# Routing of two expert layers: sums copied by columns ahead of the statistics, choice and counting by block, block 1's shift behind the placing

## What is computed

```
x = layer_norm(ALPHA * x + mixed @ w_o[layer], ln_mix_g[layer], ln_mix_b[layer])
# hier_moe(x):
probs_g = softmax(x @ w_group + b_group)              # 4 groups; the best one is taken
logits_e = (x @ w_router + b_router).reshape(T, 4, 4)
in_group = logits_e of the chosen group; softmax; top 2 of its 4 experts
gates = p_group * p_expert / (sum of the two), for 2 of the 16 experts
out = sum over experts of gate * (silu(x @ w_gate[e]) * (x @ w_up[e])) @ w_down[e]
x = layer_norm(ALPHA * x + out, ...)
```

## Time and profile before

| | us |
|---|---|
| median of 3 runs | 897.98 (897.81 to 900.09) |
| the profiled execution, its own time | 899.86 |
| its span, first to last instruction | 898.1 |
| PE busy | 879.3 |
| DVE busy | 494.2 |
| ACT busy | 406.5 |
| POOL busy | 32.3 |
| granted TensorE clock, mean | 1.000 |

### The profile page before, as it was taken

The page is one execution under the profiler, slowest core; times in us unless marked ns, Lnnn a source line. Parts: engine busy times, 40 slices in busy tenths (PEclk is TensorE's granted clock), DMA queues, the critical chain, the costliest instruction groups (busy, mean ns, idle before and its releaser), DMA issues.

```text
span 898.1 us, 13388 instructions
## 1 busy us (share of the span) xinstructions
PE 879.3 (98%) x5344; PEld 670.3 (75%) x5344; DVE 494.2 (55%) x740; ACT 406.5 (45%) x559; POOL 32.3 (4%) x73
## 2 busy tenths in 40 slices
PE   8999999999999999999999999999999999999998
PEld 7988998954543699878545445898878888888887
DVE  4798877611111775525211117656568777767566
ACT  4755655332221636653322216345646555565441
POOL 8000010000000000000000000000000000000010
PEclk9999999999999999999999999999999999999999
DMA  9924416969999494329599994654534555546611
GB/s 318 321 96 141 142 47 242 368 234 411 409 409 403 150 315 154 107 81 363 187 411 410 409 403 159 209 183 138 202 126 162 190 187 187 187 141 234 236 45 48
DMA packets 102829, 205.80 MB, mean 229 GB/s; under 512 B 6896, under 2 KB 57840, under 8 KB 102768
## 3 DMA queue, kind: packets, MB, share of 16 engines
q1 hardware_dynamic: 101184, 202.14, 62.7%
q10 hardware_dynamic: 1584, 2.81, 0.8%
HBM read 203.87 MB, written 1.05 MB: 228 GB/s over the span
## 4 chain that ended last, share of the span: by engine, by line
PE 85%; DVE 6%; ACT 3%; issue 2%; DMA 2%; SPq 1%; DVEq 0%
PE psum L723 82%; DVE w_lo L2233 2%; DMA raw<-in_a_w_in 1%; ACT w_hi L1702 1%; ACT arena L1702 1%; SPq L373 1%; DMA x_res<-in_x 1%; ACT x_slots L1702 0%; PE psum L1560 0%; PE psum L851 0%; PE psum L1247 0%; DVE xt L2254 0%; PE psum L967 0%; PE psum L1063 0%; PE psum L842 0%
## 5 line engine op out<-in xcount | busy, mean ns | idle before, releaser
L723 PE MATMUL psum<-xt,w_hi 128*128 128x256 f32 (+1 forms) x1056 | 256.2, 323 | 2.6 <-DVE w_lo L2233 1.3
L2233 DVE TENSOR_TENSOR w_lo<-raw,w_hi 128x2048 fp32r<-128x2048 f32 x88 | 200.6, 2288 | 45.9 <-ACT w_hi L1702 45.7
L723 PE MATMUL psum<-xt,w_lo 128*128 128x256 f32 x704 | 198.4, 282 | 0.0
L723 PEld LDWEIGHTS psum<-xt,w_hi 128*128 128x128 f32 x1056 | 177.3, 190 | 20.5 <-issue 1.8
L1702 ACT ACTIVATE w_hi<-raw 128x2048 fp32r<-128x2048 f32 (+1 forms) x90 | 169.8, 1892 | 36.8 <-PE psum L723 21.2
L723 PEld LDWEIGHTS psum<-xt,w_lo 128*128 128x128 f32 x704 | 134.0, 190 | 0.0
L723 PE MATMUL psum<-w_hi,xt 128*128 128x512 f32 (+1 forms) x336 | 103.8, 380 | 0.7 <-DVE w_lo L2233 0.4
L1702 ACT ACTIVATE arena<-psum 128x512 f32<-128x512 f32 (+2 forms) x74 | 43.2, 601 | 109.9 <-PE psum L723 81.6
L723 PE MATMUL psum<-hi_as_raw,x_slots 128*64 128x512 f32 x176 | 80.8, 596 | 0.0
L723 PE MATMUL psum<-lo_as_raw,x_slots 128*64 128x512 f32 x176 | 80.8, 596 | 0.0
L723 PEld LDWEIGHTS psum<-w_hi,xt 128*128 128x128 f32 x336 | 61.3, 189 | 12.6 <-issue 1.8
(11 more groups left out here) (279 smaller groups left out, 1260.4 us busy)
## 6 DMA issues: line engine op xcount, KB each, us to landing
hi_as_raw<-in_gate_up SPq DMA_DIRECT2D x44, 512.0 KB, 8.0
lo_as_raw<-in_gate_up SPq DMA_DIRECT2D x44, 512.0 KB, 9.6
raw<-in_ffn_w_up SPq DMA_DIRECT2D x44, 512.0 KB, 4.6
raw<-in_gate_up SPq DMA_DIRECT2D x40, 512.0 KB, 7.2
raw<-in_a_w_in SPq DMA_DIRECT2D x26, 512.0 KB, 7.0
raw<-in_w_down SPq DMA_DIRECT2D x24, 512.0 KB, 11.0
raw<-in_attn_w_in SPq DMA_DIRECT2D x24, 512.0 KB, 5.8
raw<-in_ffn_w_down SPq DMA_DIRECT2D x22, 512.0 KB, 4.2
```

What stands on the lines that cost most here:

```text
L723: return pe.matmul(o, l, r, start=start, stop=stop, skip_group_check=skip)
L2233: return dve.tensor_tensor(w_half(h, w_lo), w_half(h, raw), w_half(h, w_hi).bitcast(F32), ALU.subtract).then_inc(lo_split, 1)
```

## The change

Sums: ACT copies each half of a block as soon as PE has made it (`o_done` for block 0, `half_used` for each half of block 1), and DVE takes the statistics from the copy in SBUF. Scaling goes by halves. Choice: `choose(b)` runs for each block by itself. Counting: `count_first` for block 0, `count_second` for block 1. PE: block 0's logits stand inside the second product of block 1; the transposes of block 1 go by halves; layer 1 has 10 zero matmuls where there were 16. Placing: the permutation is made by block, with a semaphore for each; block 1's shift comes behind it, so block 1 is rounded (by halves) and its rest is made after that. Gather: block 0 first, then all rounded parts of block 1, then all rests. The diff, cut to its core:

```diff
@@ PE, project (layer 0) and finish_projection (layer 1)
-                for j in range(2):
-                    tm_block(base + 2 + j, 1, 1, 2 + j, xt_hi, xt_lo, False)
-                    if j == 0:
-                        turn_raw(0, 0)
+                tm_block(base + 2, 1, 1, 2, xt_hi, xt_lo, False)
+                turn_raw(0, 0)
+                def first_logits(kk):
+                    if kk == 1:
+                        raw_logits(0, 0)
+                tm_block(base + 3, 1, 1, 3, xt_hi, xt_lo, False, first_logits)
...
+                project_chunks(layer, ks, 1, (0,))
+                if layer == 1:
+                    turn_raw(1, 0)
+                project_chunks(layer, ks[:2], 1, (1,))
+                if layer == 1:
+                    raw_logits(1, 0)
+                project_chunks(layer, ks[2:], 1, (1,))
@@ PE, experts
+                def count_first():
+                    pe.wait_ge(sem("chosen"), 2 * layer + 1)
+                    ch = r_chosen[:, 0:EXPERTS]
+                    mm(psum[:, 6, 0:16], before[:], ch, True, False, skip=True)
+                    for n in range(2):
+                        mm(psum[:, 6, 16 + 16 * n:32 + 16 * n], ones[:], ch, False, False, skip=True)
+                def count_second():
+                    pe.wait_ge(sem("chosen"), 2 * layer + 2)
+                    ch = r_chosen[:, EXPERTS:2 * EXPERTS]
+                    mm(psum[:, 6, 16:32], before[:], ch, False, False, skip=True)
+                    mm(psum[:, 6, 32:48], ones[:], ch, False, True, skip=True).then_inc(sem("counted"), 1)
                 def between(share):
                     if share == 1 / 16:
-                        turn_raw(0, 1)
-                    if share == 3 / 16:
+                        turn_raw(0, 1, (0,))
+                    if share == 2 / 16:
+                        turn_raw(0, 1, (1,))
+                    if share == 4 / 16:
                         raw_logits(0, 1)
-                    if share == 9 / 16:
-                        count_chosen()
-                raw_logits(layer, 0)
+                    if share == 5 / 16:
+                        count_first()
+                    if share == 8 / 16:
+                        count_second()
                 if layer == 0:
                     fm_half("MK1", mt_hi, mt_lo, None, between)
                 else:
                     turn_raw(1, 1)
-                    keep_busy(3, 7)
                     raw_logits(1, 1)
-                    keep_busy(8, 7)
-                    count_chosen()
+                    count_first()
+                    keep_busy(5, 7)
+                    count_second()
                     keep_busy(5, 7)
...
+                pe.wait_ge(sem("first_placed"), layer + 1)
+                pe.wait_ge(sem("x_rest"), 2 * layer + 1)
+                for r, bank in enumerate(FIRST_BANKS):
+                    gather_block(0, r, bank, 0)
                 pe.wait_ge(s["perm_ready"], 1)
-                for b in range(TB):
-                    pe.wait_ge(sem("x_rest"), 2 * layer + b + 1)
+                for x_part, ready in ((x_hi, "x_rounded"), (x_lo, "x_rest")):
+                    pe.wait_ge(sem(ready), 2 * layer + 2)
                     for r, bank in enumerate(FIRST_BANKS):
-                        gather_block(0, r, bank, b)
+                        gather_block(0, r, bank, 1, (x_part,))
@@ ACT, experts
+                def round_second():
+                    for c in range(2):
+                        cs = slice(512 * c, 512 * c + 512)
+                        act.wait_ge(ln_done, 8 * layer + 2 + c + 1)
+                        last = fn(x_hi[:, 1, cs], x_res[:, 1, cs], ACT.Copy)
+                    last.then_inc(sem("x_rounded"), 1)
+                for c in range(2):
+                    raw_sum(0, c)
                 raw_out(0)
                 round_to(base)
-                raw_sum(1)
+                raw_sum(1, 0)
+                if layer:
+                    round_first()
+                raw_sum(1, 1)
                 raw_out(1)
-                round_x(0)
-                round_x(1)
+                if layer == 0:
+                    round_first()
+                round_second()
@@ DVE, mix_norm (the new order; r_less and r_more of layer 0 follow gather_stats(0))
+                split_to(h + (6, 5)[layer])
+                for c in range(2):
+                    measure(0, c)
+                gather_stats(0)
+                for c in range(2):
+                    scale(0, c)
+                shift(0)
+                measure(1, 0)
+                logits(0)
+                choose(0)
+                if layer:
+                    rest_x(0)
+                measure(1, 1)
+                gather_stats(1)
+                scale(1, 0)
+                logits(1)
+                choose(1)
+                if layer == 0:
+                    rest_x(0)
+                scale(1, 1)
+                place_slots(layer)
                 shift(1)
                 rest_x(1)
                 less_top()
@@ DVE, place_slots
-                place(layer, 0)
+                for b in range(TB):
+                    at = r_at[:, b, 0:4].rearrange("p (e o) -> p e o", o=1).to_broadcast([P, 4, SLOTS])
+                    dve.tensor_tensor(perm[:, b, :].rearrange("p (e t) -> p e t", t=SLOTS), slot_no..., at, ALU.is_equal)\
+                        .then_inc(sem(f"perm_ready{layer}" if b else "first_placed"), 1)
```

More of the change, by code:

```diff
@@ L798, in tm_half, with tm_block @@
                         after((4 * b + kk + 1) / 8)
-            def tm_block(h, half, b, bank, xh, xl, fresh=True):
+            def tm_block(h, half, b, bank, xh, xl, fresh=True, after=nothing):
                 pe.wait_ge(lo_split, h + 1)
@@ L809, in tm_block @@
                                   skip=True)
-                if b:
-                    last.then_inc(half_used, 1)
+                    if b and kk == 3:
+                        last.then_inc(half_used, 1)
+                    after(kk)
                 return last
@@ L1052, in finish_projection, with turn_raw @@
                 project_chunks(layer, O_ROWS[layer][1][3:], 0).then_inc(sem("o_done"), 1)
[L1053 to L1060, removed]
+                ks = O_ROWS[layer][1]
+                project_chunks(layer, ks, 1, (0,))
[5 more added lines that the diff above has]
+                project_chunks(layer, ks[2:], 1, (1,))
+            def turn_raw(layer, b, cs=range(2)):
+                for c in cs:
                     pe.wait_ge(sem("sum_ready"), 4 * layer + 2 * b + c + 1)
@@ L1869, in experts, with raw_sum @@
                 s = {n: sem(f"{n}{layer}") for n in MOE_SEMS}
[L1871 to L1875, removed]
+                def raw_sum(b, c):
+                    if b:
+                        act.wait_ge(half_used, AT[f"O{layer}"] + 3 + c)
+                    elif c == 0:
+                        act.wait_ge(sem("o_done"), layer + 1)
+                    fn(x_res[:, b, 512 * c:512 * c + 512], psum[:, 2 * b + c, :], ACT.Copy)\
+                        .then_inc(sem("sum_ready"), 1)
                 def raw_out(b):
@@ L2591, in mix_norm, with measure, gather_stats, scale @@
             def mix_norm(layer):
-                n, ready = 2 * layer, projected(layer)
-                sum_seen = sem("sum_seen")
-                def measure(b):
-                    for c in range(2):
-                        dve.bn_stats(stats[:, b, c, :], psum[:, 2 * b + c, :]).then_inc(sum_seen, 1)
+                n, h = 2 * layer, AT[f"O{layer}"]
+                def measure(b, c):
+                    dve.wait_ge(sem("sum_ready"), 4 * layer + 2 * b + c + 1)
+                    own.did(dve.bn_stats(stats[:, b, c, :], x_res[:, b, 512 * c:512 * c + 512]))
+                def gather_stats(b):
                     dve.nop().then_inc(drained_v, 1)
-                    dve.wait_ge(sum_seen, 4 * layer + 2 * b + 2)
+                    own.settle()
                     own.link(dve.bn_aggr(mv[:, b, :], stats[:, b, :, :].rearrange("p c s -> p (c s)")))
                     dve.tensor_scalar(var_eps[:, b:b + 1], mv[:, b, 1:2], LN_EPS, None, ALU.add).then_inc(var_ready, 1)
-                def scale(b):
+                def scale(b, c):
                     dve.wait_ge(gain_in, 32 * (n + 1))
-                    dve.wait_ge(sem("raw_turned"), 4 * layer + 2 * b + 2)
-                    own.did(dve.scalar_tensor_tensor(x_res[:, b, :], x_res[:, b, :], mv[:, b, 0:1], gain[:, 0, :],
+                    dve.wait_ge(sem("raw_turned"), 4 * layer + 2 * b + c + 1)
+                    cs = slice(512 * c, 512 * c + 512)
+                    own.did(dve.scalar_tensor_tensor(x_res[:, b, cs], x_res[:, b, cs], mv[:, b, 0:1], gain[:, 0, cs],
                                                      ALU.subtract, ALU.mult))
@@ L2629, in rest_x @@
                     rest(x_lo[:, b, :], x_res[:, b, :], x_hi[:, b, :]).then_inc(sem("x_rest"), 1)
-                ready(0)
-                measure(0)
-                scale(0)
```

(22 more changed lines are left out.)

68 lines of the change are left out of this document (32 added, 36 removed).

## The result

| | us |
|---|---|
| changed kernel, median of 6 runs | 907.87 (905.49 to 909.48) |
| kernel before beside it, 6 runs | 898.56 (896.54 to 900.29) |
| ratio, 95% interval | 1.0102, 1.0082 to 1.0121 |
| profiled execution of the changed kernel | 909.48, span 907.7 |

The change makes the kernel 1.0% slower, some 9 us, where +1.0 us was forecast; the time lies outside the range (896.4 to 900.4). The profiled spans differ by 907.7 - 898.1 = 9.6 us.

What follows compares the result with a forecast made beforehand. TensorE, busy 879.3 of 898.1 us, was taken as the bound, so a shift of the first gate-up shifts the end. Layer 0 +0.7 and layer 1 +0.3 gave +1.0 on the median 897.98: 899.0 us, range 896.4 to 900.4.

Steps and rivals of the forecast that it cites:

- the mechanism: PE's branch before the gate-up is reached only behind the wait for block 1's late rest; chance 0.65, +1.0 us.
- drain: Rival: the branch ends a fixed time behind the last gather matmul, so gains stand: 896.2 us, chance 0.12.
- run past: Rival: a matmul's own wait doesn't hold PE's sequencer, so the branch starts at 179.0 and 428.1: 896.7 us, chance 0.11.
- the fetch: Loading code at PE's branch before the gate-up: 4.0 us in layer 0 beside gain's loads, 4.18 in layer 1.
- What moves besides costs nothing: ACT's gain loads go 5 us later, with over 100 us to their use, so they were put at no cost.
- The slower rival: Gain's transfer just ahead of the fetch holds its packet: branch 6.4 us, +3.0 and +2.5, 903.5 us, chance 0.06.
- the branch eats the sooner gather: The gather ends 0.66 and 1.1 us sooner, yet the late branch makes the gate-up +0.7 and +0.3 us later.

Runs made afterwards that it cites:

- e1: Changed kernel with ACT's two gain loads moved behind the wait for all four x_slots copies: 902.42 us, ratio 1.0035.
- e3: Changed kernel with 10 zero matmuls between the gather and the branch: 905.73 us, ratio 1.0069.
- e9: Changed kernel with gain's two loads moved behind ACT's silu of the first pair: 899.80 us, ratio 1.0013.
- e11: Changed kernel with 10 zero matmuls between gather and branch and gain's loads behind the silu of the first pair: 899.69 us, ratio 1.0010.
- e13: Changed kernel with gain's first load left in place and the second behind the silu of the first pair: 900.65 us, ratio 1.0012.
- e8: Changed kernel with gain's loads behind the x_slots copies and the branch between block 0's gather and block 1's: 897.10 us, ratio 0.9987.
- e6: Changed kernel with 10 zero matmuls between gather and branch and gain's loads behind the x_slots copies: 907.00 us, ratio 1.0099.
- e5: Kernel before the change, with gain's two loads moved to where e1 has them: 899.76 us, ratio 1.0020.
- e12: As e8, the branch between the two blocks' gathers, but with gain's loads behind the silu of the first pair: 898.92 us, ratio 1.0003.
- e2: Kernel before the change, with gain's two loads moved behind ACT's wait for the placing: 903.18 us, ratio 1.0045.

## Why the prediction was wrong, step by step

**Right: the mechanism and the times up to the branch.** Block 1's rest on DVE, in both layers:
```profile
178.59 1.23 DVE L2290 TENSOR_TENSOR xt<-x_res,xt 128x1024 fp32r<-128x1024 f32 x1 [0.70 <-ACT xt L1724]
431.69 1.23 DVE L2290 TENSOR_TENSOR xt<-x_res,xt 128x1024 fp32r<-128x1024 f32 x1 [0.70 <-ACT xt L1724]
```
It ends at 178.59 + 1.23 = 179.82 (forecast 179.9), and the branch starts at 179.9: a matmul that waits does hold the sequencer. The 0.25 us that were put between the two for queued instructions were 0.1. In layer 1 the rest ends at 431.69 + 1.23 - 4.19 = 428.73 (forecast 428.9). The counting of layer 0 no longer waits, and the gather starts at 177.35 (177.2) and, less the shift, at 425.46 (425.6). The two rivals on the faster side, drain and run past, fall with this: the branch begins at the rest, and e1's shorter branch ends at no fixed distance from the gather.

**Wrong: the size of one term, the fetch.** "Gain's loads ... now run beside the fetch ... so 4.0" put at 4.0 and 4.18 us what took 6.58 and 6.74. The earlier trace rows had shown 15 packets of gain at the time of the fetch and a packet 2 us behind the branch; I read a cost of 0.33 us from it and took that for the price of loads beside a fetch. But those loads had been issued 5.8 us ahead and were nearly through. The page of the kernel before has the figure that says how long they need, the time from issue to landing of the second load, beside which I should have laid the 1.6 us that the change leaves:
```profile
gain<-in_ln_ffn_b ACTq DMA_DIRECT2D x2, 512.0 KB, 8.1
```
"What moves besides costs nothing: ACT's gain loads go 5 us later" weighed only when gain is *used*. The slower rival had mechanism and size: branch 6.4 us, gate-up +3.0 and +2.5, against a measured 6.6 to 6.7, +3.04 and +2.59. It got a chance of 0.06. A slip beside it: the bounds that the prediction names for its terms add up to -0.7 to +2.2 us, not to +0.1 to +2.0. The measured 9 us lie far outside either.

**Wrong: a term that was missing, the clock.** Neither forecast nor rival asked whether the granted clock would stay at 1.00 behind a longer gap. With the slower rival's 903.5 and 4.0 us for slower matmuls the sum is 907.5; 907.87 was measured. That is no independent check, since the 4.0 was read from the result itself; and e3's two executions at a mean clock of 1.000 (904 to 906) leave the split between gap and clock open.

**What the change is worth otherwise.** Without the loads in the way (e9, e11, e13) it is at 1.0010 to 1.0013 with intervals that hold both 1 and the forecast +1.0 us. So the forecast's claim that the branch eats the sooner gather is borne out by the gate-ups in e8's profile, where it doesn't, rather than by these times.

## What to carry to other kernels

When a change moves a step, list the DMAs that become free to start behind it, and compare their time from issue to landing with what else will use the DMA engines just then; a branch to code that isn't loaded is such a user, though no line of the kernel says so. Price a longer idle gap of TensorE twice: the gap, and the matmuls behind it in case they run at half the clock. If a branch must fetch, put it ahead of the last waits, with work queued in front of it.

## What was not expected of the hardware

- **The fetch behind a taken branch waits for loads that are already queued.** 3.3 to 3.9 us with nothing in the way, up to 6.7 with 1 MB (two loads of 512 KB) issued 1.6 us ahead, and nothing extra with one of them. The Trainium skill, "DMA: Bandwidth & Descriptors", section "Queues, rings and completion order", has each DMA engine take turns between queues, a whole packet of typically 9 to 17 descriptors at a time. By that the code would wait for one such packet of q10, not for the whole queue. The rows here count pieces of about 4 KB (46 of them are 0.17 MB) and not such packets, so they can't settle it. In layer 0 the code moved at 182 to 183, with pieces of q10 still to come; in layer 1 at 437 to 437.5, when q10's share had been at 8% and 6% for a microsecond. Why it waited so long there is open.
- **Code behind the branch comes in pieces.** A second packet stopped PE for 3.14 us in e6 and 1.34 us in e5. The Trainium skill, "Runtime: NRT & Kernel Launch", section "Instruction fetch mechanics", has the next page fetched while the current one runs; that agrees with e11, where only 0.15 us shows. In e6, where loads stood ahead of it, the fetch of the next piece was not hidden.
- **The clock behind a gap.** In the profiled executions the clock went to 0.50 behind gaps in the two routing stages of 1.34 (e5), 1.75 (e12), 2.13 (e2), 2.29 (e9), 2.35 and 2.51 (e1) and all of 2.71 us and more, and stayed at 1.00 behind 1.64 (e9), 1.73 and 2.06 (before), 2.25 and 2.67 (e13) and 2.37 (e8). It also fell in stretches where PE had no gap at all, as here in e9, during MK1 in layer 0:
```profile
172.00:174.00 2.00, 2.00 (x15) 2.00 (x14) 1.79 (x8) 0.00 (x0) 0.00 (x0) 0.69 1.02 420
174.00:176.00 2.00, 2.00 (x11) 2.00 (x11) 1.84 (x5) 0.00 (x0) 0.00 (x0) 0.50 0.84 340
```
The length of a gap does not decide it alone, and one profiled execution doesn't tell the cost of an edit to within 2 us: the runs of the kernel before range from 895.6 at a mean granted clock of 1.000 to 902.5 at 0.997. Of 103 such runs beside the experiments, the 33 at 1.000 have a median of 897.1 us and the 20 at 0.997 one of 900.6. The changed kernel's six lie at 0.990 to 0.994. What sets the low clock in the routing itself was not settled.
